# Prompt attention: a unit's transposes ahead of the next scores, and a pair's values between them

## The reference, cut to what matters

```python
qb = q.reshape(B, nb, WINDOW, A_KV, A_GROUP, A_HD).transpose(0, 1, 3, 4, 2, 5)
diff = qpos[:, :, None] - kpos[:, None, :]
mask = (diff >= 0) & (diff < WINDOW) & (kpos[:, None, :] >= 0)
o = sink_attend(qb, band(k), band(v), mask[:, None, None], sinks)
...
s = jnp.einsum('...kgqd,...ksd->...kgqs', q, k).astype(f32) * (A_HD ** -0.5)
s = jnp.where(mask, s, -jnp.inf)
mx = jnp.maximum(jnp.max(s, axis=-1), sk)
p = jnp.exp(s - mx[..., None])
den = jnp.sum(p, axis=-1) + jnp.exp(sk - mx)
return jnp.einsum('...kgqs,...ksd->...kgqd', (p / den[..., None]).astype(v.dtype), v)
```

## Time and profile before

| | before |
|---|---|
| median of 3 runs | 1730.36 us (1729.18 to 1730.45) |
| the profiled execution's own time | 1729.12 us |
| its span, first to last instruction | 1727.4 us |
| TensorE busy | 1709.3 us, 99% of the span |
| first phase of the prompt's attention | about 476 to 587 us |
| second phase | about 682 to 790 us |

### The profile page before, as it was taken

One profiled execution on the slowest core, in us unless ns is written; L12 is line 12 of the kernel. 1 busy time (PEld: TensorE's weight loads), 2 busy tenths in 40 slices (PEclk: granted clock), 3 DMA queues, 4 the chain that ended last, 5 costly groups with the idle time before them and its releaser, 6 DMA issues.

```text
span 1727.4 us, 25941 instructions
## 1 busy us (share of the span) xinstructions
PE 1709.3 (99%) x10347; PEld 1561.9 (90%) x10347; DVE 789.0 (46%) x1515; ACT 505.7 (29%) x1190; POOL 104.6 (6%) x204
## 2 busy tenths in 40 slices
PE   8999999999999999999999999999999999999998
PEld 8998998999988899889999988889999988888996
DVE  5313333442156445673525444554444454455447
ACT  6423333232245333552304311122221211112222
POOL 3001101000012100120001000000000000000001
PEclk9999999999999999999999999999999999999999
DMA  6114453833221123112421111101111011110112
GB/s 211 51 45 124 56 85 72 87 49 56 39 50 25 44 44 71 26 25 49 141 50 32 43 49 49 45 28 49 49 49 45 28 49 49 49 48 25 49 61 104
DMA packets 140891, 99.24 MB, mean 57 GB/s; under 512 B 82488, under 2 KB 132672, under 8 KB 140808
## 3 DMA queue, kind: packets, MB, share of 16 engines
q1 hardware_dynamic: 140808, 98.08, 23.8%
HBM read 88.43 MB, written 11.60 MB: 58 GB/s over the span
## 4 chain that ended last, share of the span: by engine, by line
PE 96%; issue 1%; DVE 1%; ACT 0%; DMA 0%; POOL 0%; SPq 0%; DVEq 0%; POOLq 0%; ACTq 0%
PE bank L807 35%; PE bank L1170 22%; PE bank L1143 22%; PE bank L1129 6%; PE bank L763 3%; PE bank L962 2%; PE bank L991 2%; PE bank L872 1%; PE bank L864 1%; PE bank L867 1%; PE bank L909 0%; PE bank L847 0%; PE bank L891 0%; DMA raw<-in_w_in 0%; PE bank L1031 0%
## 5 line engine op out<-in xcount | busy, mean ns | idle before, releaser
L2000 DVE TENSOR_TENSOR x<-bank,x 128x512 f32<-128x512 f32 x288 | 195.8, 690 | 139.0 <-PE bank L1170 137.3
L1143 PE MATMUL bank<-xT_hi,w_hi 128*128 128x384 f32 (+1 forms) x768 | 250.5, 326 | 1.0 <-DVE xT_lo L1608 1.0
L1143 PE MATMUL bank<-xT_hi,w_lo 128*128 128x384 f32 (+1 forms) x768 | 250.4, 326 | 0.0
L1143 PE MATMUL bank<-xT_lo,w_hi 128*128 128x384 f32 (+1 forms) x768 | 250.3, 326 | 0.0
L1170 PE MATMUL bank<-w_hi,hid_hi 128*128 128x512 f32 x576 | 227.1, 394 | 0.0
L1170 PE MATMUL bank<-w_lo,hid_hi 128*128 128x512 f32 x576 | 226.1, 392 | 0.0
L1170 PE MATMUL bank<-w_hi,hid_lo 128*128 128x512 f32 x512 | 204.1, 399 | 0.0
L807 PE MATMUL bank<-xT_hi,w_hi 128*128 128x384 f32 (+1 forms) x1008 | 195.5, 335 | 0.0
L1543 ACT ACTIVATE relu<-bank 128x384 f32<-128x384 f32 (+1 forms) x96 | 45.5, 474 | 495.2 <-PE bank L1143 495.2
L807 PE MATMUL bank<-xT_hi,w_lo 128*128 128x384 f32 (+1 forms) x1008 | 186.3, 326 | 0.0
L807 PE MATMUL bank<-xT_lo,w_hi 128*128 128x384 f32 (+1 forms) x1008 | 186.1, 326 | 0.0
(11 more groups left out here) (219 smaller groups left out, 2193.6 us busy)
## 6 DMA issues: line engine op xcount, KB each, us to landing
raw<-in_w_in SPq DMA_DIRECT2D x64, 256.0 KB, 4.6
raw<-in_w_up SPq DMA_DIRECT2D x16, 1024.0 KB, 5.5
raw<-in_w_down SPq DMA_DIRECT2D x16, 1024.0 KB, 5.0
raw<-in_w_in SPq DMA_DIRECT2D x9, 1024.0 KB, 5.8
xin<-in_x_prompt SPq DMA_DIRECT2D x8, 512.0 KB, 4.3
bc<-gate_rows SPq DMA_DIRECT2D x32, 128.0 KB, 5.8
Cin<-in_state_C SPq DMA_DIRECT2D x4, 1024.0 KB, 8.0
out<-Cin SPq DMA_DIRECT2D x16, 256.0 KB, 8.8
```

Source lines behind the costliest of these rows:

```text
L1143: last = nc.tensor.matmul(bank[n % 4][:, 0:cn], w[:, slot, k * WCOLS + tile * P:k * WCOLS + (tile + 1) * P], x[:, k, c0:c0 + cn], start=(s ...
L2000: nc.vector.tensor_tensor(v, bank[4 + d % 4][:, :], v, ALU.add).then_inc(free_v, 1)
```

## The change

In each step of a phase TensorE now does the transposes of unit n first, then the values of the pair before (if n is even and not 0), then the scores of unit n + 2, then fill n + 1. The last pair's values stand behind the last fill, as before. ACT's list follows: `at_out` stands behind the next unit's `at_copy` and ahead of `at_exps`, where it stood behind the fill. The lists of DVE, POOL and SP stay as they are.

```diff
@@ at TensorE's prompt()
                 for n in range(HALF):
                     u = u0 + n
+                    at_transposes(u)
+                    if n and n % 2 == 0:
+                        at_values(u // 2 - 1)
                     if n + 2 < HALF:
                         at_scores(u + 2)
-                    at_transposes(u)
                     fill(fills[n + 1])
-                    if n % 2:
-                        at_values(u // 2)
+                at_values((u0 + HALF) // 2 - 1)
@@ at ScalarE's prompt_act()
                     at_copy(u)
+                    if n and n % 2 == 0:
+                        at_out(u // 2 - 1)
                     if n + 2 < HALF:
                         at_exps(u + 2)
                     fill(fills[n + 1])
-                    if n % 2:
-                        at_out(u // 2)
+                at_out((u0 + HALF) // 2 - 1)
```

## The result

The changed kernel takes 1735.17 us (median of 7 runs, 1734.78 to 1736.97) against 1730.36 for the kernel before (7 runs): 1.003 times, 95% interval 1.002 to 1.004. That is 4.8 us slower, where 5.0 were forecast. The profiled executions are 5.7 us apart (1734.78 against 1729.12, spans 1733.1 against 1727.4).

The account below looks back on a forecast made before the run. TensorE was taken as the bound, busy 1709.3 of 1727.4 us. 1.7 + 2.2 + 1.1 = 5.0 us made the profiled execution 1734.1; with the median 1.24 above, 1735.4, range 1731.6 to 1738.2.

Parts of the forecast that it names:

- Term 1: Seams between kinds of TensorE work in 30 groups of both phases: about 0.06 us dearer each, 1.7 us taken.
- plain count of row groups: At TensorE's seams, counting only overlapping row groups: two before and two afterwards, so the order costs 0, whole sum 3.3.
- Faster: Rival at TensorE's seams: a group pays one seam instead of two, 30 groups win 3.0 to 4.5 us; chance 0.04.
- Term 2: Ahead of fills 4 and 10, both phases: transposes wait for a division delayed by a weight split, 4 x 0.56 = 2.2 us.
- Only the seams: Rival: waits for the division and at the second phase's start are mostly covered; 1732.5 us, chance 0.20.
- Term 3: Start of the second phase: scores no longer cover the wait for the division, so the fill starts later, 1.1 us.
- The collision of POOL with the mask: Rival at fills 7 and 13 of each phase: POOL holds up the mask, division late, +2.4 us, 1738.0; chance 0.12.
- no cost: ACT's copy and exponentials, `at_out`, POOL's selects and DMA: slack suffices; otherwise TensorE waits a few tenths each time.

Follow-up runs that it names:

- the last experiment: The changed kernel with the scores of two units paired, so groups ahead of even fills hold transposes alone; 1.0057 times the kernel before.

## Why the prediction was right

The forecast was 1735.4, and 5.0 us as the sum of three terms. The phases measured 5.70 in the profile, 1.5 + 3.0 + 1.2.

- **Term 1, the order itself**: 1.7 us forecast, 1.4 to 1.5 measured. The first phase with the late split moved has it alone: 0.72 to 0.73 for 15 groups. The transposes were right (0.53); the fills gained 0.07 where I had 0.05 (0.10 at the end less 0.05 at the start, from a single instance), so a group costs 0.048 and not 0.06 to 0.07. My plain count of row groups, by which term 1 would be 0, falls, and so does the rival *Faster*, in which the new order had the cheaper seams.
- **Term 2, the waits behind the late split**: the right four places and the right cause, but 2.2 us forecast and 3.0 measured. Two steps were undersized. I had the split keep its distance to the fill's end, read as the start of what follows. But what follows now starts 0.1 sooner against the fill's last matmul, since the fill gains 0.10 at that seam, and ACT's reading, which the split follows, does not: the mask started 2.81 into the group and not 2.72. So each wait is 0.66, the last, behind a gating operation, 0.77. And transposes that had to wait take 0.59, not 0.53. The rival *Only the seams* falls with these four waits.
- **Term 3, the start of the second phase**: 1.1 us beside 0.1 in term 1, 1.24 measured together. Its counterfactual was richer than the prediction had it: take the wait away and 0.6 of it comes back one fill later.
- **The collision of POOL with the mask** did not happen. No 320-column fill behind values is followed by a wait (the group at 523.33, with the next transposes at 530.41, and three more), nor is fill 1 of either phase. DVE's work in the first window fell from 63.40 to 57.40 us, because POOL is out of its sink operations' way, as forecast (0.15 at 508.43 where the earlier trace rows had 0.60): its two operations with the sinks (L1786 and L1788 of before) fell from 11.0 to 5.1 us in the first phase.
- **The bounds of "no cost"** held: no wait of TensorE for ACT's copy, its reading of fills or POOL was added.

That the forecast met the median to 0.2 is partly luck. Measured against the phases the sum of 5.0 was 0.7 short: 0.8 too little in term 2, a few tenths too much in term 1. Against that stands the 1.24 us by which I put the median above the profiled execution, as it was for the kernel before; in the changed kernel it was 0.39. So the medians moved by 4.8 and the profiled executions by 5.7. One execution differs from another mostly in the lead-in, ahead of anything changed: the first scores start between 476.0 and 477.6 in these traces.

## What to carry to other kernels

When the bound engine is busy to 99%, read its timeline from start to start and price the seams between kinds of work, as a "busy" of modelled ends hides them. An order with fewer changes of shape can win where a mere exchange of places loses: here the scores in pairs gave 0.2%, and the new order cost 0.3%. Moving a consumer ahead of its cover is safe only against the latest producer and the shortest cover, so look for the rare slot (a split, a gating operation, the start of a phase, a shorter fill) and not for the usual one. A wait that is taken away should be followed to the next consumer before its price is credited.

## What the runs showed of the hardware that I had not expected

**The clock.** In the last experiment one wait of 1.9 us, and the four transposes behind it, were followed by values at half speed:

```profile
716.01 0.66 PE L763 MATMUL bank<-ident,prob 128*128 128x128 f32 x4 [1.77 <-DVE prob L1799]
716.60 3.55 PE L991 MATMUL bank<-pT,avn 128*64 128x512 f32 x8
720.08 2.04 PE L962 MATMUL bank<-akT,aqT 64*128 64x256 f32 x16
```

```profile
716.00:720.10 4.10, 4.09 (x14) 1.14 (x14) 0.49 (x1) 0.91 (x5) 0.00 (x0) 0.60 1.24 230
```

The values take 3.48 instead of 1.87, and the mean granted clock of the stretch is 0.60: most of it at 1.2 GHz. The same wait at 509.88 and at 550.22 (idle 1.77) and a longer one of the same trace at 759.01 (1.89) were followed by values of 1.87. So a wait of this length may cost nearly its double, or not; in the trace of the changed kernel the waits of 0.5 to 1.2 us did not.

The clock also goes with the spread of the lead-in. From 5 to 20 us of the span the mean granted clock is 1.00 in the last experiment, 0.89 in the kernel before and 0.77 in the one with scores in pairs, and the first scores start at 476.01, 476.26 and 477.53. That experiment's profiled execution is the fastest of its five, and its median is 9.9 us above that of before; how often the clock fell in the other four no trace shows.

**POOL beside DVE.** POOL's first select took 1.20 us where it takes 0.63 to 0.64 elsewhere (513.22 in before), when DVE's 1.23 us subtraction of two SBUF tensors ran (505.44 and 505.96 above). In the earlier trace rows it was DVE that had to wait, for POOL. Either of them can be the one that is held up.
